# The order of TensorE's work in one recurrent step: the four groups of scores for the next step, placed one by one between groups of small products

## The chip, the cores and the metric

The kernel runs on one core of a Trainium2 chip. The metric is the device time of one execution in microseconds (us): the median of several runs, and, for one more execution, the time and the trace that the hardware profiler took.

## What is computed

One encoder layer over two sequences (1024 and 256 tokens, 1280 in all, width 1024): an input projection, a rotary attention branch, an RWKV-7 branch that reads the tokens forwards and backwards, a gated merge, and a feed-forward block with two layer norms. The part that the change touches is the recurrence of the RWKV-7 branch, for 16 heads of 64 in two directions:

```python
def step(S, inp):
    r_t, w_t, kh_t, ak_t, v_t, kt_t = inp
    sk = jnp.einsum('bhvk,bhk->bhv', S, kh_t)
    S = S * w_t[:, :, None, :] - sk[..., None] * ak_t[:, :, None, :] + v_t[..., None] * kt_t[:, :, None, :]
    return S, jnp.einsum('bhvk,bhk->bhv', S, r_t)
```

The kernel doesn't go token by token. It takes chunks of 64 tokens, in which the recurrence becomes products of 64x64 matrices and the inverse of a triangular matrix, and carries only the state S from chunk to chunk.

## The kernel before

The layer is done in stages, each with its own semaphores and a barrier at its end. The recurrence is `state_stage` (L1145 to L1445), some 457 us of the 3401 us. It walks 40 steps (`NSTEP`): 20 chunks for each half of the heads. One step works on 8 units (`U`), four forward and four backward, each a pair of heads. Nothing plans the order: each engine's instructions are written out by hand, and semaphores hold them against each other.

In one step g TensorE (PE) does, in this order, with 16 products in each group unless said otherwise (the trace counts an fp32 product as two MATMUL and two LDWEIGHTS):

- L1269 and L1235, mixed, 32 products: state times keys into bank BB, and the centred values of step g + 1 into bank UB;
- L1284: one corner of the inverse (called x here), into bank CB, which ACT evicts as Wt (L1349);
- L1293 and L1296, mixed, 32 products: the outputs' part from the state (bank OB) and the rest of BB; its last instruction raises `b_ready`, on which ACT evicts Bs (L1356) and the sync queue loads the operands of step g + 3 (L942, called at L1205, two DMAs of 640 KB);
- L1304: the second corner (n), on which DVE builds the inverse NF (L1392 and L1393, two of each);
- `scores(g + 1, 0)` and `scores(g + 1, 1)` (L1228), 4 products of 192 columns each;
- `heads` with NF and Bs (L1243), called u here; it ends in the eviction of X on ACT (L1361) and DVE (L1436);
- `scores(g + 1, 2)`;
- `heads` with KTt and X (L1243), called s: the change of the state, which DVE adds and scales (L1403, L1410);
- `scores(g + 1, 3)`;
- `heads` with X and SC (L1243), called o: the outputs, which DVE moves to oR (L1421, L1423).

A group of scores uses one of two pairs of PSUM banks, so `scores` waits until DVE's `mask` (L1380) and ACT's `transposes` (L1334) of the group two before are done. DVE goes through `inverse(g)`, `mask(g+1, 0)`, `mask(g+1, 1)`, the X eviction, `mask(g+1, 2)`, `state(g)`, `mask(g+1, 3)`, `outputs(g)`. ACT goes through Wt, the two halves of the values (`evict`, L1339), Bs, transposes 0 and 1, X, transposes 2 and 3. The sync queue loads the corners of the inverse for four further steps at every fourth step (L1195), behind `nf_done`.

Of the kernel before, what the change touches and what calls it, by code (L numbers as in the profile page):

```python
# [7 lines left out]
ALU = mybir.AluOpType  # L8
# [1136 lines left out]
def state_stage(nc, hbm, cst, pv, oR, ring, ahead, pool, ub_ready, xT, oa_ready):  # L1145

    with Stage(nc, "rc") as st:
        NSTEP = 2 * NCH
# [5 lines left out]
        NF = st.sb("NF", 128, U, CH)  # L1154
# [4 lines left out]
        ps = st.psum()  # L1159
# [18 lines left out]
        def nblk(g):  # L1178
            return 5 * (g // NCH) + (g % NCH) // 4
# [35 lines left out]
        def _(pe):  # L1215
# [42 lines left out]
            for g in range(NSTEP):  # L1258
                x, sc, v = ub[g % 3], SC[g % 2], X[g % 2]
                if g + 1 < NSTEP:  # L1260
                    pe.wait_ge(ub_ready[(g + 1) % 3], 32 * ((g + 1) // 3) + 32)
                    if g:
                        pe.wait_ge(u_done, 2 * g)
                    else:
                        pe.wait_ge(v_done, 2)
                pe.wait_ge(s_done, 2 * g + 2)
                for u in range(U):
                    for h in range(2):
                        last = pe.matmul(ps[half(h), BB, CH * u:CH * u + CH], x[half(h), u, 3 * CH:4 * CH], S[half(h), u, :],  # L1269
                                         start=u == 0, stop=True, skip_group_check=True)  # L1270
                    if u == U - 1:
                        last.then_inc(bd_ready, 1)
                    if g + 1 < NSTEP:
                        values(g + 1, u)
                pe.wait_ge(masked, 4 * g + 4)
                pe.wait_ge(nb_ready[nblk(g) % 3], 64 * (nblk(g) // 3) + 64)
                if g:
                    pe.wait_ge(nf_done, 4 * g)
                n_, r_ = corners(nb, g), corners(rb, g)
                for u in ALTERNATE:  # L1280
                    for h in range(2):
                        d = u // 4
                        i, o = (64 * h, 64 * h + 32) if d == 0 else (64 * h + 32, 64 * h)
                        last = pe.matmul(ps[o:o + 32, CB, 32 * u:32 * u + 32], sc[i:i + 32, u, h, o % 64:o % 64 + 32],  # L1284
                                         r_[d][i:i + 32, u % 4, :], start=True, stop=True)
                last.then_inc(x_ready, 1)
                pe.wait_ge(v_done, 2 * g + 2)
                pe.wait_ge(bd_ready, g + 1)
                if g:
                    pe.wait_ge(o_done, 2 * g)  # L1290
                for u in range(U):
                    for h in range(2):
                        pe.matmul(ps[half(h), OB, CH * u:CH * u + CH], S[half(h), u, :], x[half(h), u, 4 * CH:5 * CH],  # L1293
                                  start=u == 0, stop=True, skip_group_check=True)
                    for h in range(2):
                        last = pe.matmul(ps[half(h), BB, CH * u:CH * u + CH], sc[other(h), u, h, 0:CH], v[other(h), u, h, :],  # L1296
                                         start=False, stop=True, skip_group_check=True)
                last.then_inc(b_ready, 1)
                pe.wait_ge(w_done, g + 1)
                for u in ALTERNATE:  # L1300
                    for h in range(2):
                        d = u // 4
                        i, o = (64 * h + 32, 64 * h) if d == 0 else (64 * h, 64 * h + 32)
                        last = pe.matmul(ps[o:o + 32, CB, 256 + 32 * u:256 + 32 * u + 32], Wt[i:i + 32, u, :],  # L1304
                                         n_[d][i:i + 32, u % 4, :], start=True, stop=True)
                last.then_inc(n_ready, 1)
                if g + 1 < NSTEP:
                    scores(g + 1, 0)
                    scores(g + 1, 1)
                    pe.wait_ge(v_done, 2 * g + 4)  # L1310
                pe.wait_ge(b_done, g + 1)
                pe.wait_ge(nf_done, 4 * g + 4)
                heads(ps, UB, lambda u, h: NF[half(h), u, :], lambda u, h: Bs[half(h), u, :], True).then_inc(u_ready, 1)
                if g + 1 < NSTEP:
                    scores(g + 1, 2)
                pe.wait_ge(u_done, 2 * g + 2)
                if not last_of(g):
                    pe.wait_ge(kt_done, 4 * g + 4)
                    heads(ps, BB, lambda u, h: KTt[g % 2][:, u, h, :], lambda u, h: v[:, u, h, :], True).then_inc(s_ready, 1)
                if g + 1 < NSTEP:  # L1320
                    scores(g + 1, 3)
                heads(ps, OB, lambda u, h: v[:, u, h, :], lambda u, h: sc[:, u, h, CH:2 * CH], False).then_inc(o_ready, 1)

        def score_view(ps, q, c, n):
# [4 lines left out]
        @block.scalar  # L1329
        def _(act):  # L1330
            def transposes(g, q):
                n = 4 * g + q
                act.wait_ge(masked, n + 1)
                act.activation(KTt[g % 2][:, 2 * q:2 * q + 2, :, :], score_view(ps, q, 128, CH), ACT.Copy).then_inc(kt_done, 1)  # L1334

            def evict(g):
                for h in range(2):
                    rows = slice(64 * h, 64 * h + 64)
                    act.activation(X[g % 2][rows, :, 1 - h, :], ps[rows, UB, :].rearrange("p (u n) -> p u n", n=CH),  # L1339
                                   ACT.Copy).then_inc(v_done, 1)  # L1340

            for q in range(4):
                act.wait_ge(sc_ready, q + 1)
                transposes(0, q)
            act.wait_ge(v_ready, 1)
            evict(0)
            for g in range(NSTEP):
                act.wait_ge(x_ready, g + 1)
                act.activation(Wt[:, :, :], ps[:, CB, 0:256].rearrange("p (u n) -> p u n", n=32), ACT.Copy, scale=-1.0).then_inc(w_done, 1)  # L1349
                if g + 1 < NSTEP:  # L1350
                    act.wait_ge(v_ready, g + 2)
                    if g:
                        act.wait_ge(o_ready, g)
                    evict(g + 1)
                act.wait_ge(b_ready, g + 1)
                act.activation(Bs[:, :, :], ps[:, BB, :].rearrange("p (u n) -> p u n", n=CH), ACT.Copy).then_inc(b_done, 1)  # L1356
                if g + 1 < NSTEP:
                    for q in range(2):
                        transposes(g + 1, q)
                act.wait_ge(u_ready, g + 1)  # L1360
                act.activation(X[g % 2][0:64, :, 0, :], ps[0:64, UB, :].rearrange("p (u n) -> p u n", n=CH),  # L1361
                               ACT.Copy, scale=-1.0).then_inc(u_done, 1)
                if g + 1 < NSTEP:
                    transposes(g + 1, 2)
                    transposes(g + 1, 3)

        @block.gpsimd
# [5 lines left out]
        def _(dve):  # L1373
# [6 lines left out]
                dve.tensor_tensor(SC[g % 2][:, 2 * q:2 * q + 2, :, :], score_view(ps, q, 0, 2 * CH),  # L1380
                                  cst[:, at:at + 128].unsqueeze(1).unsqueeze(1).broadcast_to([128, 2, 2, 128]), ALU.mult).then_inc(masked, 1)

            def inverse(g):
                n = corners(nb, g)
                dve.wait_ge(nb_ready[nblk(g) % 3], 64 * (nblk(g) // 3) + 64)
                dve.wait_ge(n_ready, g + 1)
                if g:
                    dve.wait_ge(u_ready, g)
                for d in range(2):
                    us, mine = slice(4 * d, 4 * d + 4), 1 - d  # L1390
                    z = ps[:, CB, 256 + 128 * d:384 + 128 * d].rearrange("p (u n) -> p u n", n=32)
                    dve.tensor_scalar(NF[:, us, 32 * d:32 * d + 32], n[d], sel[d], None, ALU.mult).then_inc(nf_done, 1)  # L1392
                    dve.scalar_tensor_tensor(NF[:, us, 32 * mine:32 * mine + 32], n[d], sel[mine], z, ALU.mult, ALU.add).then_inc(nf_done, 1)  # L1393

            def state(g):
# [32 lines left out]
            for q in range(4):  # L1428
                mask(0, q)
            for g in range(NSTEP):  # L1430
                inverse(g)
                if g + 1 < NSTEP:
                    mask(g + 1, 0)
                    mask(g + 1, 1)
                dve.wait_ge(u_ready, g + 1)
                dve.tensor_scalar(X[g % 2][64:128, :, 1, :], ps[64:128, UB, :].rearrange("p (u n) -> p u n", n=CH),  # L1436
                                  -1.0, None, ALU.mult).then_inc(u_done, 1)
                if g + 1 < NSTEP:
                    mask(g + 1, 2)
                state(g)  # L1440
                if g + 1 < NSTEP:
                    mask(g + 1, 3)
                if g:
                    dve.wait_ge(o_done, 2 * g)
                outputs(g)  # L1445
# [727 lines left out]
```

## Time and profile before

| | us |
|---|---|
| median of 3 runs | 3413.84 |
| the 3 runs | 3404.06, 3413.84, 3415.73 |
| the profiled execution | 3403.2 |
| its span in the trace | 3401.3 |
| PE busy in the span | 3227.4 (95%) |
| DVE busy | 1803.5 (53%) |
| ACT busy | 1035.7 (30%) |
| mean granted TensorE clock | 0.986 |

Times in the trace count from the start of the span. An idle stretch that the profile calls "issue" is one in which the engine waited for no other engine's work. PE and PEld are the MATMULs and the LDWEIGHTS of the same engine.

### The profile page before, as it was taken

The page shows a single profiled execution, that of the slowest core. Times are in us where ns is not written, and L with a number is a line of the kernel's source. Part 1 is how long each engine was busy: PE and PEld are TensorE (multiplying, and loading weights), DVE is VectorE, ACT ScalarE, POOL GpSimd, SP SyncE. Part 2 cuts the span into 40 slices and gives each one's busy share as a digit, 9 for nine tenths or more (in the row PEclk, how much of TensorE's full clock was granted, in tenths as well). Part 3 has the DMA queues.
Part 4 walks back from the last instruction along what each step waited for, and adds up shares of the span by engine and source line. Part 5 has one row for each costly group of instructions (what it writes and reads, how often), then busy time and mean ns, then how long its engine had stood idle before and what let it go on. Part 6 is the DMA issues. An engine that isn't in the chain of part 4 may idle for free. (4 is left out here: it accounts for less than half of the span.)

```text
span 3401.3 us, 59585 instructions
## 1 busy us (share of the span) xinstructions
PE 3227.4 (95%) x25992; PEld 2055.7 (60%) x25992; DVE 1803.5 (53%) x3002; ACT 1035.7 (30%) x1590; POOL 2.5 (0%) x13
## 2 busy tenths in 40 slices
PE   9999999999999899888888999998999999999997
PEld 4565564555555455577777554565666666666665
DVE  1437662677677478055555332155545445645445
ACT  2336651343333133233333452002321121221111
POOL 0000000000000000000000000000000000000000
PEclk9999999999999999999999999998999999999998
DMA  3221111344434423355443223211111211222211
GB/s 136 62 68 36 38 38 42 120 135 167 152 120 150 157 102 138 133 188 164 147 150 114 82 87 138 81 50 50 62 62 62 81 62 64 73 87 75 68 62 62
DMA packets 211234, 328.48 MB, mean 97 GB/s; under 512 B 51232, under 2 KB 168224, under 8 KB 205856
## 3 DMA queue, kind: packets, MB, share of 16 engines
q1 hardware_dynamic: 210976, 324.67, 28.7%
q8 instruction: 207, 3.39, 0.4%
q14 instruction: 51, 0.42, 0.0%
HBM read 221.74 MB, written 96.34 MB: 94 GB/s over the span
## 5 line engine op out<-in xcount | busy, mean ns | idle before, releaser
L620 PE MATMUL ra_ps<-xT,ring 128*128 128x512 f32 (+1 forms) x1152 | 429.8, 526 | 0.0
L1742 PE MATMUL tl_ps<-merged,pool 128*128 128x320 f32 x1440 | 407.4, 435 | 6.4 <-PEq L108 3.9
L1742 PEld LDWEIGHTS tl_ps<-merged,pool 128*128 128x128 f32 x1440 | 275.0, 191 | 124.0 <-issue 12.1
L620 PEld LDWEIGHTS ra_ps<-xT,ring 128*128 128x128 f32 x1152 | 214.3, 190 | 198.9 <-issue 189.3
L1935 DVE TENSOR_TENSOR oR<-tl_ps,oR 128x320 f32<-128x320 f32 x416 | 201.9, 489 | 151.2 <-PE tl_ps L1742 149.0
L1058 PE MATMUL rg_ps<-xT,ring 128*128 128x512 f32 (+1 forms) x720 | 265.7, 524 | 11.9 <-PEq L108 11.9
L1742 PE MATMUL tl_ps<-tl_Th,pool 128*128 128x320 f32 x720 | 205.7, 437 | 6.1 <-issue 6.1
L1058 PEld LDWEIGHTS rg_ps<-xT,ring 128*128 128x128 f32 x720 | 134.7, 191 | 122.7 <-issue 117.2
L1823 ACT ACTIVATE ring<-tl_ps 128x320 f32<-128x320 f32 x96 | 41.9, 437 | 528.7 <-PE tl_ps L1742 528.6
L1742 PE MATMUL tl_ps<-xT,pool 128*128 128x320 f32 x640 | 183.2, 433 | 0.0
L1941 DVE TENSOR_TENSOR merged<-tl_ps,ring 128x320 f32<-128x320 f32 x96 | 47.2, 491 | 254.0 <-PE tl_ps L1742 135.4
L1742 PEld LDWEIGHTS tl_ps<-tl_Th,pool 128*128 128x128 f32 x720 | 138.5, 193 | 64.7 <-issue 8.7
L1742 PE MATMUL tl_ps<-merged,tl_sums 128*128 128x320 f32 x544 | 163.2, 439 | 12.8 <-DVE oR L1935 7.8
L280 PE MATMUL at_ps<-xT,ring 128*128 128x512 f32 (+1 forms) x432 | 159.1, 521 | 0.0
L1228 PE MATMUL rc_ps<-pool 64*128 64x192 f32 x1280 | 142.5, 349 | 11.7 <-POOL pool L1370 6.9
L1742 PEld LDWEIGHTS tl_ps<-xT,pool 128*128 128x128 f32 x640 | 122.0, 191 | 51.1 <-issue 0.8
L1520 PE MATMUL mg_ps<-xT,ring 128*128 128x512 f32 (+1 forms) x384 | 144.2, 529 | 1.9 <-PEq L108 1.9
L305 PE MATMUL at_ps<-at_qk 128*128 128x512 f32 (+1 forms) x288 | 135.7, 594 | 8.3 <-ACT at_p L372 7.9
L1520 PE MATMUL mg_ps<-oR,ring 128*128 128x512 f32 (+1 forms) x384 | 139.4, 526 | 2.9 <-DVE oR L1573 2.9
L317 PE MATMUL at_ps<-at_turned,at_v 32*128 32x256 f32 x2176 | 137.0, 386 | 4.0 <-DVE at_ot L456 4.0
L1742 PEld LDWEIGHTS tl_ps<-merged,tl_sums 128*128 128x128 f32 x544 | 102.9, 192 | 62.0 <-issue 22.4
L317 PEld LDWEIGHTS at_ps<-at_turned,at_v 32*128 32x128 f32 x2176 | 108.3, 184 | 49.1 <-issue 43.4
(239 smaller groups left out, 4654.2 us busy)
## 6 DMA issues: line engine op xcount, KB each, us to landing
pool<-ub SPq DMA_DIRECT2D x80, 640.0 KB, 5.3
ub<-ra_ub SPq DMA_DIRECT2D x32, 1280.0 KB, 5.3
pool<-in_w_ff SPq DMA_DIRECT2D x32, 1024.0 KB, 4.7
pool<-in_w_ff SPq DMA_DIRECT2D x64, 512.0 KB, 3.5
ring<-in_w_in SPq DMA_DIRECT2D x39, 512.0 KB, 3.7
xT<-in_xT SPq DMA_DIRECT2D x16, 640.0 KB, 8.2
ub<-ra_v SPq DMA_DIRECT2D x16, 640.0 KB, 6.5
mg_gate<-gates SPq DMA_DIRECT2D x16, 640.0 KB, 3.9
```

What stands on the lines that cost most here:

```text
L280: last = pe.matmul(ps[:, z_bank(i) + j, 0:n], w[:, i % 3, 128 * k:128 * k + 128], xT[:, k, t0:t0 + n], start=(k == 0), stop=(k == KT - 1))
L305: last = pe.matmul(ps[:, 2 * (t % 2) + b // 512, 0:n], qk[:, h, t0:t0 + 128], qk[:, QH + h // (QH // KVH), k0 + b:k0 + b + n], start=True, ...
L317: last = pe.matmul(ps[:, 4 + i, 0:256], values_of(g, i, j), pT[g % 2][32 * i:32 * i + 32, j].rearrange("p t q -> p (t q)"), start=(j == 0) ...
L620: last = pe.matmul(ps[:, bank + j, 0:n], w[c][:, 128 * i:128 * i + 128], xT[:, i, t0:t0 + n], start=(i == 0), stop=(i == KT - 1))
L1058: last = pe.matmul(ps[:, 3 * (b % 2) + j, 0:n], w[b % 3][:, 128 * i:128 * i + 128], xT[:, i, t0:t0 + n], start=(i == 0), stop=(i == KT - 1))
L1228: last = pe.matmul(ps[:, 4 + 2 * (q % 2) + h, 192 * j:192 * j + 192], x[rows, 2 * q + j, CH:3 * CH], x[rows, 2 * q + j, 3 * CH:6 * CH], st ...
L1520: last = pe.matmul(ps[:, 3 * (i % 2) + j, 0:n], w[i % 2][:, 128 * k:128 * k + 128], src[:, k, t0:t0 + n], start=(k == 0), stop=(k == KT - 1))
L1742: last = pe.matmul(bank(n, b), lhs(k), rhs(k), start=(fresh and k == 0), stop=(k == d - 1), skip_group_check=True)
L1823: act.activation(cp[n % 2][:, c, :], bank(n, b), ACT.Copy).then_inc(done, 1)
L1935: dve.tensor_tensor(y, bank(n, b), y, ALU.add).then_inc(done, 1)
L1941: dve.tensor_tensor(hidden(n, i, j), bank(n, b), cp[n % 2][:, c, :], ALU.add).then_inc(done, 1)
```

## The change

Within a step, PE's groups stand in another order. x moves ahead of the group BB with values. The groups of scores for step g + 1 stand apart: 0 ahead of x, 1 between BB with values and OB with BB, 2 between n and u, 3 between u and s. s and o now follow each other, and so do x and the BB group. One explicit wait on `ub_ready` goes away, because `scores(g + 1, 0)` has the same. No product is added or removed.

DVE and ACT follow this order. `inverse(g)` is split: the two operations on the own corners (L1392), which need nothing of this step's products, go first; the two on the other corners (L1393) go behind the masks 0 and 1. Masks 2 and 3 come one place earlier, transposes 0 and 1 stand around `evict`, transposes 2 ahead of X.

```diff
             for g in range(NSTEP):
                 x, sc, v = ub[g % 3], SC[g % 2], X[g % 2]
                 if g + 1 < NSTEP:
-                    pe.wait_ge(ub_ready[(g + 1) % 3], 32 * ((g + 1) // 3) + 32)
+                    scores(g + 1, 0)
+                pe.wait_ge(masked, 4 * g + 4)
+                pe.wait_ge(nb_ready[nblk(g) % 3], 64 * (nblk(g) // 3) + 64)
+                if g:
+                    pe.wait_ge(nf_done, 4 * g)
+                n_, r_ = corners(nb, g), corners(rb, g)
+                for u in ALTERNATE:
...
+                last.then_inc(x_ready, 1)
+                if g + 1 < NSTEP:
                     if g:
                         pe.wait_ge(u_done, 2 * g)
...
                         last.then_inc(bd_ready, 1)
                     if g + 1 < NSTEP:
                         values(g + 1, u)
-                pe.wait_ge(masked, 4 * g + 4)
...
-                last.then_inc(x_ready, 1)
+                if g + 1 < NSTEP:
+                    scores(g + 1, 1)
                 pe.wait_ge(v_done, 2 * g + 2)
...
                 last.then_inc(n_ready, 1)
                 if g + 1 < NSTEP:
-                    scores(g + 1, 0)
-                    scores(g + 1, 1)
+                    scores(g + 1, 2)
                     pe.wait_ge(v_done, 2 * g + 4)
...
                 if g + 1 < NSTEP:
-                    scores(g + 1, 2)
+                    scores(g + 1, 3)
                 pe.wait_ge(u_done, 2 * g + 2)
...
-                if g + 1 < NSTEP:
-                    scores(g + 1, 3)
                 heads(ps, OB, lambda u, h: v[:, u, h, :], lambda u, h: sc[:, u, h, CH:2 * CH], False).then_inc(o_ready, 1)
...
                 if g + 1 < NSTEP:
+                    transposes(g + 1, 0)
                     act.wait_ge(v_ready, g + 2)
...
                     evict(g + 1)
+                    transposes(g + 1, 1)
                 act.wait_ge(b_ready, g + 1)
...
-                    for q in range(2):
-                        transposes(g + 1, q)
+                    transposes(g + 1, 2)
...
                 if g + 1 < NSTEP:
-                    transposes(g + 1, 2)
                     transposes(g + 1, 3)
...
-                inverse(g)
+                own_corners(g)
                 if g + 1 < NSTEP:
                     mask(g + 1, 0)
                     mask(g + 1, 1)
+                other_corners(g)
+                if g + 1 < NSTEP:
+                    mask(g + 1, 2)
                 dve.wait_ge(u_ready, g + 1)
...
                 if g + 1 < NSTEP:
-                    mask(g + 1, 2)
+                    mask(g + 1, 3)
                 state(g)
-                if g + 1 < NSTEP:
-                    mask(g + 1, 3)
```

## Rows read from the trace of the kernel before

**Rows 1.** The page's first part: busy time, share of the span, instructions.
```profile
PE 3227.4 (95%) x25992; PEld 2055.7 (60%) x25992; DVE 1803.5 (53%) x3002; ACT 1035.7 (30%) x1590; POOL 2.5 (0%) x13
```
**Rows 2.** Windows, steps 1 to 38: length, busy time (count) per engine, clock, DMA share, GB/s.
```profile
1456.20:1883.66 427.46, 371.94 (x12068) 321.86 (x12065) 237.99 (x530) 155.49 (x342) 0.00 (x0) 1.00 0.45 145
```
**Rows 3.** Waits of PE and PEld in these 38 steps: us in total, times, longest.
```profile
PE rc_ps L1296 <- issue: 16.2, 12, 1.7
...
PE rc_ps L1304 <- issue: 13.0, 9, 1.8
...
PE rc_ps L1293 <- issue: 8.6, 6, 1.8
...
PEld rc_ps L1243 <- DVE rc_X L1436: 8.4, 35, 0.2
```
**Rows 4.** Timeline of PE, one step: start, us, line, count, idle before.
```profile
1603.27 0.45 PE L1304 MATMUL rc_ps<-rc_nb,rc_Wt 32*32 32x32 f32 x32
1603.65 1.57 PE L1228 MATMUL rc_ps<-pool 64*128 64x192 f32 x16
1605.15 1.15 PE L1243 MATMUL rc_ps<-rc_Bs,rc_NF 64*64 64x64 f32 x32
1606.23 0.92 PE L1228 MATMUL rc_ps<-pool 64*128 64x192 f32 x8
1607.10 1.15 PE L1243 MATMUL rc_ps<-rc_X,rc_KT 128*64 128x64 f32 x32
1608.18 0.92 PE L1228 MATMUL rc_ps<-pool 64*128 64x192 f32 x8
1609.03 1.15 PE L1243 MATMUL rc_ps<-rc_SC,rc_X 128*64 128x64 f32 x32
1610.11 0.27 PE L1269 MATMUL rc_ps<-rc_S,pool 64*64 64x64 f32 x2
...
1611.20 0.45 PE L1284 MATMUL rc_ps<-rc_rb,rc_SC 32*32 32x32 f32 x32
1611.59 0.27 PE L1293 MATMUL rc_ps<-pool,rc_S 64*64 64x64 f32 x2
```
**Rows 5.** Windows from the end of one stall to the end of the next.
```profile
1467.52:1470.98 3.46, 2.20 (x127) 1.96 (x127) 0.00 (x0) 1.45 (x3) 0.00 (x0) 1.00 0.02 5
1490.81:1494.25 3.44, 2.16 (x127) 1.92 (x127) 0.00 (x0) 1.45 (x3) 0.00 (x0) 1.00 0.32 128
...
1757.81:1764.40 6.59, 5.82 (x125) 4.88 (x125) 5.03 (x11) 1.63 (x5) 0.00 (x0) 1.00 1.05 327
```
**Rows 6.** DMA queues in the 38 steps: packets, MB, share of 16 engines.
```profile
q8 instruction: 95, 1.56, 1.4%
```
**Rows 7.** DMA queues, 1468.60 to 1470.95 us.
```profile
q8 instruction: 1, 0.02, 2.8%
```
**Rows 8.** DMA queues, 1757.90 to 1762.10 us: all of them.
```profile
q1 hardware_dynamic: 1178, 1.37, 98.9%
q14 instruction: 1, 0.01, 0.5%
```
**Rows 9.** DMA queues, 1762.10 to 1764.35 us.
```profile
q8 instruction: 1, 0.02, 2.6%
```
**Rows 10.** Timeline of the sync queue: issues of the operand loads, 1755 to 1775 us.
```profile
1756.80 0.91 SPq L942 DMA_DIRECT2D pool<-ub  x2
```
**Rows 11.** Timeline of the sync queue, 1602 to 1605 us.
```profile
1603.37 0.92 SPq L942 DMA_DIRECT2D pool<-ub  x2
```
**Rows 12.** DMA queues, 1604.20 to 1604.40 us.
```profile
q8 instruction: 1, 0.02, 44.5%
```
**Rows 13.** Timeline of DVE in the step of rows 4.
```profile
1604.06 0.34 DVE L1393 SCALAR_TENSOR_TENSOR rc_NF<-rc_nb,cst,rc_ps 128x128 f32<-128x128 f32 x1
...
1604.52 0.34 DVE L1393 SCALAR_TENSOR_TENSOR rc_NF<-rc_nb,cst,rc_ps 128x128 f32<-128x128 f32 x1
...
1606.35 0.69 DVE L1436 TENSOR_SCALAR rc_X<-rc_ps 64x512 f32<-64x512 f32 x1 [0.29 <-PE rc_ps L1243]
...
1609.02 0.76 DVE L1410 TENSOR_TENSOR rc_S<-rc_t,pv 128x256 f32<-128x256 f32 x2
```

More of the change, by code:

```diff
@@ L1260, in _ @@
                 if g + 1 < NSTEP:
-                    pe.wait_ge(ub_ready[(g + 1) % 3], 32 * ((g + 1) // 3) + 32)
+                    scores(g + 1, 0)
[5 more added lines that the diff above has]
+                for u in ALTERNATE:
+                    for h in range(2):
+                        d = u // 4
+                        i, o = (64 * h, 64 * h + 32) if d == 0 else (64 * h + 32, 64 * h)
+                        last = pe.matmul(ps[o:o + 32, CB, 32 * u:32 * u + 32], sc[i:i + 32, u, h, o % 64:o % 64 + 32],
+                                         r_[d][i:i + 32, u % 4, :], start=True, stop=True)
+                last.then_inc(x_ready, 1)
+                if g + 1 < NSTEP:
                     if g:
@@ L1274, in _ @@
                         values(g + 1, u)
-                pe.wait_ge(masked, 4 * g + 4)
[L1276 to L1285, printed above, removed]
-                last.then_inc(x_ready, 1)
+                if g + 1 < NSTEP:
+                    scores(g + 1, 1)
                 pe.wait_ge(v_done, 2 * g + 2)
@@ L1381, in mask, with own_corners @@
                                   cst[:, at:at + 128].unsqueeze(1).unsqueeze(1).broadcast_to([128, 2, 2, 128]), ALU.mult).then_inc(masked, 1)
-            def inverse(g):
+            def own_corners(g):
                 n = corners(nb, g)
                 dve.wait_ge(nb_ready[nblk(g) % 3], 64 * (nblk(g) // 3) + 64)
-                dve.wait_ge(n_ready, g + 1)
                 if g:
@@ L1389, in inverse, with other_corners @@
                 for d in range(2):
+                    dve.tensor_scalar(NF[:, 4 * d:4 * d + 4, 32 * d:32 * d + 32], n[d], sel[d], None, ALU.mult).then_inc(nf_done, 1)
+            def other_corners(g):
+                n = corners(nb, g)
+                dve.wait_ge(n_ready, g + 1)
+                for d in range(2):
                     us, mine = slice(4 * d, 4 * d + 4), 1 - d
                     z = ps[:, CB, 256 + 128 * d:384 + 128 * d].rearrange("p (u n) -> p u n", n=32)
-                    dve.tensor_scalar(NF[:, us, 32 * d:32 * d + 32], n[d], sel[d], None, ALU.mult).then_inc(nf_done, 1)
                     dve.scalar_tensor_tensor(NF[:, us, 32 * mine:32 * mine + 32], n[d], sel[mine], z, ALU.mult, ALU.add).then_inc(nf_done, 1)
```

## Prediction

> **What bounds the kernel now.** I read the page's busy shares first: PE is busy for 95% of the span, DVE for 53% [rows 1], so time is won or lost on PE. The change touches only the recurrent stage. There the windows view gives 427.46 us for 38 steps, 11.25 us each, with PE busy for 371.94 of them at full clock [rows 2]: 55.5 us are idle. The view of waits says on what: nothing that another engine owed. Most of it is "issue", ahead of L1296, L1304 and L1293, at up to 1.8 us a time, and the only engine that PE's weight loads wait for is DVE's X eviction, 8.4 us in 35 times [rows 3].
>
> The timeline of a step without a stall gives each group's price as the distance of two starts [rows 4]: n 0.38, scores 0 and 1 together 1.50, u 1.08, scores 2 0.87, s 1.08, scores 3 0.85, o 1.08, BB with values 1.09, x 0.39, and OB with BB 1.09, taken as for the other mixed group, which has as many products. The sum is 9.41 us. The real step is 11.25, so about 1.84 us of each, 70 us of the stage, are stalls.
>
> What they are: from the end of one stall to the end of the next PE ran 127 MATMULs and 127 LDWEIGHTS, which with two waits are 256 instructions [rows 5], and the 38 steps have 95 packets on the DMA queue of instructions, 1.56 MB or 16 KB each [rows 6], which is 256 instructions of 64 bytes. PE is waiting for its own program. Two such stalls ended 3.44 and 3.46 us apart [rows 5], with one packet between them [rows 7]: entering a block asks for the next, and that is there some 3.5 us later. A step has 640 instructions and about 8 waits, 2.5 blocks.
>
> The Trainium skill's page Runtime: NRT & Kernel Launch, section Instruction fetch mechanics, also has 16 KB blocks fetched while the current one runs, and calls the cost of a boundary "mostly hidden". The trace agrees on the block and not on the cost. If it were hidden here, a step would take its 9.41 us, and of this change only the fourth tail (below) would be left, some 8 us slower.
>
> Second, a refill can be late. At 1756.80 the loads of step g + 3 are issued [rows 10]; PE enters a block at 1757.81, and its refill doesn't start before 1762.10: up to there only the load moves, on 98.9% of the DMA engines, and then the one packet of 16 KB comes [rows 8, 9]. That block took 6.59 us [rows 5]. A refill asked for at 1603.27, 0.1 us ahead of a load's issue [rows 4, 11], started 0.8 to 1.0 us behind that issue [rows 12]. Free of load it would start 1.1 to 1.3 us after the entry and be usable 2.3 us after that. So one that would start up to 1.0 us after the issue goes through, and one that would start at 2.2 us (1757.81 + 1.2 - 1756.80) waits until 5.3 us and is usable at 7.7. Where in between the line lies, the trace doesn't show.
>
> **The change part by part.**
>
> *The groups themselves.* No product is added. But a group of scores costs 0.64 us for its products and 0.22 until the next kind can start: two together take 1.50, one alone 0.86 [rows 4]. Before there are three such tails in a step, after it four: +0.22 us, 9.63 us without stalls. From below, the tail could cost nothing ahead of the small 32x32 products of x: no row has scores ahead of them. I take 0.2, since all three followers in the trace show it.
>
> *The removed wait* on PE is free, since the same wait stands in scores 0, and the loads were issued more than two steps earlier.
>
> *The waits that move.* u now has only scores 2 ahead of it (0.86) where it had 1.50. It waits for DVE: the second L1393 ended at 1604.86, 1.59 after n started, with four operations [rows 4, 13]. With two of them left behind n, the end comes some 0.4 us earlier, about 1.2 after n's start, where scores 2 ends at 0.38 + 0.86 = 1.24. That is covered by nothing to spare; its price lies between 0 and 0.1 us a step. s waits for X behind one group of scores as before (0.2 us at most, as now). The state is done at 1609.78, 0.33 ahead of its reader [rows 4, 13]; after the change o, scores 0 and x stand there, 2.3 us, so this cover grows and gives nothing, since PE isn't waiting there now. DVE's masks 0 and 1 stand ahead of the other corners, but score group 1 ends 1.5 us ahead of n's end, and a mask takes 0.7. On ACT transposes 0 and 1 stand ahead of Bs; they wait for the same masks and are done ahead of `b_ready` or within 0.2 us of it, and Bs is needed 1.2 us behind it. The loads hang on `b_ready` and those of the corners on `nf_done`, as before.
>
> *The stalls.* This is what the change really moves. In the dense stretch a block of 256 instructions before takes 2.0 us (BB with values, x, half of OB with BB), against 3.5 for the refill: 1.5 us of stall. After, scores 1 stands in it, and the same stretch takes 2.7 to 2.8: some 0.75 less. But the groups that follow the load have lost what the dense stretch won. From the end of OB with BB to the start of the next BB group before there are 325 instructions and 6.84 us; after, up to the start of x, there are 310 and 6.25 us, and then the dense groups start. A refill that the load holds up is usable at 7.7 us. Before, PE can be near that point with 256 instructions; after it gets there sooner.
>
> One walk by these two rules shows it. A block is entered 90 instructions behind OB with BB, in the shadow of the load. Before: the next block is wanted at 7.0 and is there at 7.7, stall 0.7; the one after is wanted 2.0 later, stall 1.5; two blocks on, 1.3; then 0 and 1.5 (5.0 us in three steps). After: wanted at 6.45, stall 1.25; then 0.7; 0.3 and 0.4; 0.9 and 0.75 (4.3 us in three steps). Three steps before: 28.2 + 5.0 = 33.2. After: 28.9 + 4.3 = 33.2. What the dense stretch gains, the held-up refill and the fourth tail take.
>
> I carried the same two rules through 39 steps for 32 positions of the first block boundary, with the hold lasting to 6.6 us in those steps that also load corners or attention outputs. Before gives 11.18 us a step, where the trace has 11.25; that is the check of the rules. After depends on the line between 1.0 and 2.2 us that the trace leaves open: up to 1.7 it gives 11.40 to 11.42 (+0.23), at 1.9 it gives 11.19 (0), at 2.17 it gives 10.95 (-0.23). With the line evenly likely between the ends, the mean is +0.14. Times 39 steps that is +5.5 us, with ends of -9 and +9.
>
> **The sum.** The profiled execution has 3403.2 us, 10.6 below the median of 3413.84; it is the fastest of the four times, whose spread is 12. With +5.5 its time is 3409. Against the median I forecast 3419.
>
> **The rivals.**
>
> *A, clearly faster: the load doesn't hold these refills.* If each refill takes 3.5 us wherever it is asked for, the rules give 10.55 before and 10.03 after: -0.52 us a step, -20 us, 3394. For it: the dense stretch is the largest stall in rows 3, and the change thins just that. Against it: before would be at 10.55, not 11.25, and rows 8 to 10 show the hold. A part of this is possible, where the line lies at 2.2 or a held refill gets through earlier: -10 to -12, 3402. The Trainium skill's page DMA: Bandwidth & Descriptors, section Queues, rings and completion order, has each DMA engine take turns between its queues packet by packet; by that a refill wouldn't wait for a whole load. Rows 8 and 9 show one that did.
>
> *B, clearly slower: the shadow of the load begins early, and u waits.* The line is at 1.7 or below (+0.23), and u pays its 0.1 for the corners: +0.33 us a step, +13, 3427. It decides from the point where the other corners end over 1.24 us after n's start.
>
> *C, DVE or ACT in a new order becomes the bound.* DVE is busy 238 of 427 us, ACT 155 [rows 2]. Were a mask or Bs 0.5 us late in each step, +20, 3434. I see no place for it: little chance.
>
> *D, nothing of this matters,* stalls are as before and the tail is absorbed in them: 3414, inside my forecast.
>
> **How the numbers follow.** About 0.3% (10 us) is what a measurement of this kernel can tell from no change. Forecast and D (within it): 0.45. A, full or in part: 0.24. B and C: 0.31. The range holds the forecast, the part of A down to half its price and B: 3398 to 3434.
>
> **What would show it.** In the trace after: the step without a stall is 9.6 us; scores stand in four places with 0.86 each; the "issue" waits ahead of L1296, L1293 and L1304 shrink by about half, and those ahead of L1284, L1269, L1235 and of o grow by about as much; the 38 steps take 427 to 437 us. If the latter don't grow, A is right. If u's weight loads wait for DVE L1393, B's part is right. The prediction is wrong if the stage's time moves by over 12 us, or if other stages do.

## The result, and the profile after

The changed kernel takes 3418.26 us (median of 20 runs, 3411.13 to 3426.45). The kernel before, run beside it on the same chip, takes 3410.24 (median of 20 runs, 3404.06 to 3426.57). The ratio is 1.0028 with an interval of 1.0019 to 1.0036: slower by 0.28%, some 8 to 10 us. That is just under the 0.3% that I had named as the limit of what can be told apart, and the interval lies clear of 1.

The profiled execution took 3417.64 us, with a span of 3415.8. Its page's first part, to be held against [rows 1]:

```profile
PE 3236.4 (95%) x25992; PEld 2062.6 (60%) x25992; DVE 1810.0 (53%) x3002; ACT 1041.2 (30%) x1590; POOL 2.5 (0%) x13
```

The same instructions ran, as they should. Now the recurrent stage, from the barrier ahead of it to the one behind it, in the windows view (stretch, length, busy time and count of PE, PEld, DVE, ACT, POOL, granted clock, DMA share, GB/s). First before, then after:

```profile
1433.70:1894.00 460.30, 395.58 (x12672) 342.24 (x12672) 251.16 (x559) 163.86 (x360) 1.72 (x3) 0.98 0.46 148
```
```profile
1431.30:1915.40 484.10, 412.80 (x12672) 350.75 (x12672) 257.27 (x559) 169.31 (x360) 1.72 (x3) 0.95 0.44 141
...
1458.78:1909.08 450.30, 388.34 (x12020) 330.42 (x12017) 242.62 (x527) 158.95 (x338) 0.00 (x0) 0.95 0.43 138
```

The stage is 23.8 us longer in this pair of profiles, and the other stages together 9.3 shorter, which makes the 14.5 between the spans. The other stages run the same code in all 14 profiles below, and what is left of the span beside the recurrent stage ranges from 2931.7 to 2942.2 us in them, so the 9.3 is scatter. The second row of after is 38 steps, from n of one to n of another: 450.3 us, where [rows 2] has 427.46. The last figure but two is what surprises: the granted clock is 0.95, where [rows 2] has 1.00. I come back to it; it isn't in my sum at all.

The waits of PE in those 38 steps (us in total, times, longest), against [rows 3]. The lines have moved: L1271 is x, L1282 BB, L1235 values, L1296 OB with L1299, L1307 n, L1243 u, s and o.

```profile
PE rc_ps L1282 <- issue: 12.5, 9, 3.6
PE rc_ps L1235 <- issue: 8.2, 5, 3.4
PE rc_ps L1299 <- issue: 7.5, 11, 1.5
PE rc_ps L1271 <- issue: 7.4, 8, 1.3
PE rc_ps L1228 <- issue: 6.9, 4, 3.1
PE rc_ps L1296 <- issue: 6.3, 5, 2.5
PE rc_ps L1243 <- issue: 5.8, 7, 1.6
PE rc_ps L1307 <- issue: 5.3, 5, 1.6
```

The lines of before that [rows 3] leaves out, from the same stretch:

```profile
PE rc_ps L1269 <- issue: 6.6, 5, 2.3
PE rc_ps L1228 <- issue: 4.5, 6, 1.2
PE rc_ps L1284 <- issue: 3.5, 4, 1.3
PE rc_ps L1235 <- issue: 1.5, 3, 0.9
PE rc_ps L1243 <- issue: 0.9, 1, 0.9
```

In [rows 3] three lines had 37.8 us of the 54.8 that this view puts down to "issue". L1299, L1307 and L1296 answer to them and fell from 16.2, 13.0 and 8.6 to 7.5, 5.3 and 6.3. x, BB, values and the L1243 groups rose from 3.5, 6.6, 1.5 and 0.9 to 7.4, 12.5, 8.2 and 5.8. So the first fell by 18.7 us and the others rose by 21.4, as the prediction had named it ("by about as much"). But the longest stalls are now 3.1 to 3.6 us, ahead of BB, values and scores, where the longest of before in this stretch was 2.3.

A step without a stall, as the timeline of PE shows it (start, us, line, count):

```profile
1591.15 0.45 PE L1307 MATMUL rc_ps<-rc_nb,rc_Wt 32*32 32x32 f32 x32
1591.53 0.92 PE L1228 MATMUL rc_ps<-pool 64*128 64x192 f32 x8
1592.43 1.15 PE L1243 MATMUL rc_ps<-rc_Bs,rc_NF 64*64 64x64 f32 x32
1593.51 0.92 PE L1228 MATMUL rc_ps<-pool 64*128 64x192 f32 x8
1594.37 1.15 PE L1243 MATMUL rc_ps<-rc_X,rc_KT 128*64 128x64 f32 x32
1595.35 1.10 PE L1243 MATMUL rc_ps<-rc_SC,rc_X 128*64 128x64 f32 x32
1596.38 0.92 PE L1228 MATMUL rc_ps<-pool 64*128 64x192 f32 x8
1597.23 0.45 PE L1271 MATMUL rc_ps<-rc_rb,rc_SC 32*32 32x32 f32 x32
```

The scores stand alone, 0.85 to 0.90 each. s and o now follow each other directly and take 2.01 together (1594.37 to 1596.38), where each took 1.08 in [rows 4]. Over the groups of all steps that had no stall in them, a step without stalls comes to 9.50 us, where before has 9.41.

*How the stalls were split.* In every profile below I counted PE's instructions in blocks of 256 from the known boundary. The boundary falls on the same place of the count in all of them, since the instructions are as many. For each block I noted when it was entered, when the next packet on the queue of instructions started, and how long PE then stood at the next boundary. A refill whose packet started over 1.6 us after the entry is called held, whatever held it; the others are called free. The stage of before has 24.4 us of stalls behind held refills and 45.5 behind the others. The stage of after has 62.8 and 14.1. So of the stalls that the change was to thin, two thirds are gone, and the others have grown 2.6-fold.

One of the long ones. The sync queue issues the loads, PE enters a block at 1552.21, and only the operand loads' queue moves up to 1558.20 (DMA queues of 1552.30 to 1558.20 us, then of 1558.20 to 1560.50; packets, MB, share of 16 engines):

```profile
1549.65 1.56 SPq L942 DMA_DIRECT2D pool<-ub  x2
1551.26 0.51 SPq L1210 DMA_DIRECT2D xT<-o_att  x1
```
```profile
q1 hardware_dynamic: 910, 1.57, 77.9%
...
q8 instruction: 1, 0.02, 2.5%
```
```profile
1560.55 0.37 PE L1282 MATMUL rc_ps<-rc_S,pool 64*64 64x64 f32 x2 [3.58 <-issue]
```

This is the picture of [rows 8, 9], with the attention load queued as well, and with the dense groups right at its end. PE stands for 3.58 us, inside BB.

### The profile page after: what moved, and what is told of

The parts are those of the page before. It is cut to its first block and busy times, and to the rows that moved or that the text cites. A ratio compares the mean times of both kernels' runs of the same rounds, so it can differ in the third digit from the quotient of the medians.

```text
span 3415.8 us, 59584 instructions
## 1 busy us (share of the span) xinstructions
PE 3236.4 (95%) x25992; PEld 2062.6 (60%) x25992; DVE 1810.0 (53%) x3002; ACT 1041.2 (30%) x1590; POOL 2.5 (0%) x13
## 3 DMA queue, kind: packets, MB, share of 16 engines
q1 hardware_dynamic: 210976, 324.67, 28.5%
## 5 line engine op out<-in xcount | busy, mean ns | idle before, releaser
L1747 PEld LDWEIGHTS tl_ps<-merged,pool 128*128 128x128 f32 x1440 | 275.3, 192 | 123.4 <-issue 11.9
L1380 DVE TENSOR_TENSOR rc_SC<-rc_ps,cst 128x512 f32<-128x512 f32 x160 | 110.3, 689 | 117.3 <-PE rc_ps L1228 117.3
L1228 PE MATMUL rc_ps<-pool 64*128 64x192 f32 x1280 | 157.3, 365 | 14.3 <-POOL pool L1370 6.9
```

The lines of the kernel that those rows point to most:

```text
L1228: last = pe.matmul(ps[:, 4 + 2 * (q % 2) + h, 192 * j:192 * j + 192], x[rows, 2 * q + j, CH:3 * CH], x[rows, 2 * q + j, 3 * CH:6 * CH], st ...
L1747: last = pe.matmul(bank(n, b), lhs(k), rhs(k), start=(fresh and k == 0), stop=(k == d - 1), skip_group_check=True)
```

## The experiments

All times are medians, and the ratio behind each is to the kernel before, run beside it on the same chip. The table gives, from one profile of each kernel, the stage's length, the two kinds of stalls in it, the stalls over 2 us, and the length of the spells at a granted clock of 0.50 that begin in it. A profile is one execution: those of before_paced and after_early took 3418.0 and 3380.6 us, 7.5 over and 9.1 under their medians, so their rows are less typical than the others.

| kernel | median us | stage | held | others | over 2 us | clock at 0.50, us |
|---|---|---|---|---|---|---|
| before | 3410.2 | 460.3 | 24.4 | 45.5 | 2 | 17.0 |
| before_again | (3412.6) | 472.2 | 29.0 | 42.4 | 4 | 37.4 |
| after | 3418.3 | 484.1 | 62.8 | 14.1 | 9 | 44.2 |
| after_again | (3418.5) | 481.6 | 61.7 | 17.9 | 9 | 30.6 |
| before_cut | 3364.9 | 423.2 | 0.2 | 36.2 | 0 | 13.6 |
| after_cut | 3346.0 | 409.5 | 6.4 | 13.9 | 1 | 3.4 |
| before_half | 3425.9 | 491.8 | 43.0 | 20.4 | 3 | 47.6 |
| before_paced | 3410.5 | 473.6 | 40.5 | 28.5 | 11 | 51.0 |
| after_paced | 3380.0 | 436.8 | 29.9 | 14.0 | 2 | 6.8 |
| after_spread | 3380.4 | 439.9 | 27.8 | 18.7 | 2 | 6.8 |
| after_poolq | 3429.8 | 489.5 | 67.9 | 14.5 | 14 | 40.8 |
| after_fine | 3378.2 | 436.3 | 28.4 | 16.4 | 2 | 3.4 |
| before_early | 3407.3 | 464.0 | 33.5 | 30.5 | 8 | 40.8 |
| after_early | 3389.7 | 443.3 | 34.8 | 15.4 | 3 | 6.8 |

In brackets: one execution.

**Take the load away: before_cut and after_cut.** Both orders of PE, but the loads of the steps move almost no bytes: the operands' (shown), and in the same way those of the corners and of the attention outputs. The recurrence's result is left out, and its instructions stay.

```diff
...
-                    load_units(sp, hbm, ub[g % 3], g + 3, ub_ready[g % 3])
+                    for d in range(2):
+                        sp.dma_start(ub[g % 3][0:16, 4 * d, 0:5 * CH],
+                                     hbm["ub"][0, d, 0:16, chunk_of(g % 3, d), :]).then_inc(ub_ready[g % 3], 16)
...
```

> The kernel before, with the sync queue's DMAs inside the 40 steps cut to 16 partitions (operands of later steps, corners, attention outputs), the operands and corners of the first three steps used again, and the new state multiplied by a zero column, so that nothing grows: the recurrence's result is left out, its instructions stay. Theory (refills of PE's program held behind the loads): no refill is held, a step takes 10.55 us instead of 11.24, so some 27 us less than the kernel before; the stalls behind BB with values (1.5 us each in OB with BB and n) stay. Rival (the stalls have nothing to do with the loads): the time of the kernel before within 5 us.

> The same cut on the changed kernel. Theory: with no refill held, the thinner dense stretch pays at last: 9.86 us a step against 10.55, so 27 us LESS than before_cut, some 50 less than the kernel before. Rival (the change costs time by its fourth tail of a scores group and by waits for DVE and ACT): 5 to 15 us MORE than before_cut.

Measured: before_cut 3364.91 (ratio 0.986, 0.9843 to 0.9877), 43 us under before; after_cut 3346.04 (0.9806, 0.9789 to 0.9823), 19 under before_cut and 72 under after. Their stages in the windows view:

```profile
1436.60:1859.80 423.20, 387.03 (x12672) 336.94 (x12672) 250.70 (x559) 163.63 (x360) 1.72 (x3) 0.98 0.09 24
```
```profile
1435.90:1845.40 409.50, 391.00 (x12672) 334.62 (x12672) 256.99 (x559) 167.37 (x360) 1.72 (x3) 0.99 0.09 25
```

The DMA share is down from 0.46 to 0.09, held stalls are gone in the first and down to 6.4 us in the second (what holds those I didn't find), and now the change pays: 19 us. With the loads in place it costs 8 to 10. So the loads take some 28 us off what the new order brings by itself. That is the core of my theory, and the direction of the theory holds on both sides. Both sizes were off. Before lost 43 instead of 27. One part of that is the stalls behind free refills, which shrank too (45.5 to 36.2), and which my fixed 3.5 us didn't allow; with the held ones that makes 33.5, and the rest isn't explained. The change brought 19 instead of 27, which is what the prediction had put under rival A (20).

**Spread the load: before_paced and after_paced.** Four pieces of 320 KB, one each behind OB with BB, u, o and the next BB group.

```diff
-                    load_units(sp, hbm, ub[g % 3], g + 3, ub_ready[g % 3])
+                    piece(g, 0)
+                    sp.wait_ge(u_ready, g + 1)
+                    piece(g, 1)
+                    sp.wait_ge(o_ready, g + 1)
+                    piece(g, 2)
+                    sp.wait_ge(bd_ready, g + 2)
+                    piece(g, 3)
```

> The kernel before, complete, but each step's operand load is issued in four DMAs of 320 KB, at the ends of OB with BB, u, o and the next BB group, in place of two of 640 KB at the first of these. Theory: a refill then waits for one piece of some 1.2 us, not for 4; steps of 10.6 to 10.9 us, 13 to 25 us less than the kernel before. Rival: the kernel before within 5 us.

> The same pacing on the changed kernel, complete. Theory: steps of 9.9 to 10.4 us, 35 to 50 us less than the kernel before, and the granted clock stays at full in the stage since no stall is over 2 us. Rival: the changed kernel's 3418 within 5 us.

Measured: before_paced 3410.52 (1.0006, 0.9993 to 1.0018), after_paced 3380.0 (0.9906, 0.9891 to 0.9921). The windows view of the two:

```profile
1436.80:1910.40 473.60, 408.90 (x12672) 354.09 (x12672) 252.04 (x559) 164.87 (x360) 1.73 (x3) 0.95 0.50 144
```
```profile
1435.40:1872.20 436.80, 396.60 (x12672) 337.56 (x12672) 257.17 (x559) 168.56 (x360) 1.72 (x3) 0.99 0.54 156
```

The same bytes, with after in 47 us less of stage than when they come at once (38 in the medians), and before with no gain. For after the theory held in kind and was too high in size: I expected 35 to 50 us under before and steps of 9.9 to 10.4 us, and got 28 by the medians (32 by the ratio) and 38 steps in 406.7 us, 10.7 each. There were still two stalls over 2 us and 6.8 us at 0.50, where I expected none. For before it missed: I expected a gain and found none. The split shows what happened. The stalls behind free refills fell from 45.5 to 28.5, but the held ones rose from 24.4 to 40.5, eleven of them over 2 us, and the sum hardly moved (69.9 and 69.0). My reading is that the pieces behind o and BB come just where the dense stretch of before needs its refills, and that nothing long stands in that stretch to cover a late one; before_early below moves them and gains only 4 us, so this reading isn't shown.

**Half of the change: before_half.** The kernel before with only score group 0 moved, from behind n to between x and OB with BB. DVE and ACT keep their order.

```diff
+                if g + 1 < NSTEP:
+                    scores(g + 1, 0)
...
-                    scores(g + 1, 0)
```

> The kernel before with one part of the change alone: only scores 0 of the next step moves, from behind n to between x and OB with BB; ACT and DVE keep their order. Theory: stalls behind refills that no load holds fall (45.5 us before, 25 to 35 here), those behind held refills grow (24.4 us before, 35 to 50 here), for 310 instructions are left behind the load instead of 325; a step is 11.4 to 11.6 us, the time 5 to 15 us over the kernel before. Rival (stalls alone follow the dense stretch): both kinds of stall fall and the time is 5 to 10 us under the kernel before.

Measured: 3425.85 beside 3410.99 (1.0044, 1.0028 to 1.006), 15 us over before and slower than the whole change. That is the upper end of what I expected, but not for my reason alone. Its waits of PE name a cause that neither before nor after has:

```profile
PE rc_ps L1243 <- DVE rc_NF L1394: 12.5, 30, 0.4
...
PE rc_ps L1269 <- issue: 10.4, 10, 3.0
```

One group of scores is left between n and u, as in the whole change, but DVE still has all four operations on the corners behind n. So u waits for them in 30 of the steps, 12.5 us in total. In the whole change two of the four have gone ahead, and u waits for NF only once, in the first step (waits of after in its stage):

```profile
PEld rc_ps L1243 <- DVE rc_X L1443: 9.5, 38, 0.9
PEld rc_ps L1296 <- ACT rc_X L1339: 8.6, 33, 0.4
...
PE rc_ps L1271 <- DVE rc_SC L1380: 1.5, 1, 1.5
...
PE rc_ps L1243 <- DVE rc_NF L1397: 0.8, 1, 0.8
```

So this kernel doesn't isolate the refills, as I had meant it to. Held stalls of 43.0 are within the 35 to 50 that I expected and the others, 20.4, under the 25 to 35; what each part is worth in time can't be read from it. What it shows is that the wait of rival B exists, and that the split of `inverse` is what the whole change avoids it with.

**Spread the corner loads too: after_spread.** after_paced, with one of the four corner loads in each of four steps, issued behind the piece that follows u.

```diff
...
-                if g % 4 == 3 and nblk(g) + 3 < 10:
-                    sp.wait_ge(nf_done, 4 * g + 4)
-                    load_inverse(nblk(g) + 3)
+                    if g >= 3 and nblk(g - 3) + 3 < 10:
+                        h = g - 3 - (g - 3) % 4 + 3
+                        sp.wait_ge(nf_done, 4 * h + 4)
+                        load_inverse(nblk(h) + 3, (g - 3) % 4)
...
```

> after_paced, and the loads of the inverse's corners too are taken apart: one DMA of 256 KB in each of four steps in place of four behind each other in every fourth. Complete. Theory: steps 3, 7, ... 27 have the longest holds (packets up to 9 us behind the load's issue in the changed kernel), so these seven steps lose 1 to 2 us each: 3370 against 3380, no half clock in the stage. Rival (what is left is stalls of 3.5 us refills and tails only): 3380 within 3 us.

Measured: 3380.37 (0.9912, 0.9899 to 0.9925), the same as after_paced, where the theory had 3370. The rival was right: once the operand load is spread, the corner loads cost nothing that can be measured.

**The same two kernels again.** To see what one profile is worth.

> The kernel before once more, for its trace: the stage between its barriers took 460.3 us with 2 spells at half clock that are not its end. If these are typical, it is within 5 us of that; theory two (the first trace of before was a lucky one) has it at 465 to 475 us.

> The changed kernel once more, for its trace: the stage took 484.1 us, with 10 spells at half clock, 44 us. Theory (long stalls behind held refills let the clock drop): again 8 to 12 such spells and 478 to 488 us. If it was chance, 3 or fewer spells and some 470 us.

Measured: 3412.62 and 3418.51, 5.9 apart. The stage of before_again in the windows view:

```profile
1435.90:1908.10 472.20, 406.10 (x12672) 351.36 (x12672) 252.50 (x559) 164.69 (x360) 1.72 (x3) 0.96 0.46 145
```

It is 11.9 us longer than in the first profile of the same kernel, with nearly the same stalls (71.4 against 69.9). What differs is the clock: spells of 37.4 us at a granted 0.50 instead of 17.0, in six more of 3.4 us each, and the same instructions keep PE busy for 406.10 us instead of 395.58. So one spell costs some 1.7 us (the 10.4 that the stalls leave, over six), and the spells vary from run to run. The profile on which I built the prediction was a lucky one; against the second one the stage of after_again (481.6) is only 9.4 longer. In this second pair the stalls make +8.2 (held +32.7, others -24.5), the groups +3.5 (below) and two spells fewer some -3.4, which is 8.3 of the 9.4. after_again has 7 spells that begin in the stage, where the theory wanted 8 to 12; its stage lies in the range that I gave.

**Another engine's queue: after_poolq.** The operand loads of after, issued by GpSimd behind the same `b_ready`, and no longer by the sync engine.

```diff
...
+            for g in range(NSTEP - 3):
+                pool.wait_ge(b_ready, g + 1)
+                load_units(pool, hbm, ub[g % 3], g + 3, later[g % 3])
```

> The changed kernel, complete, with the operand loads of the 40 steps issued from GpSimd instead of the sync queue, at the same semaphore. It asks whose the hold is. If the DMA engines work off what is queued before the refill, whoever queued it: refills held as in the changed kernel, time 3410 to 3430. If only the sync queue's DMAs hold the refill: stalls behind held refills fall from 62 us to under 20 and the time to 3370 to 3385.

Measured: 3429.82 beside 3411.71 (1.005, 1.0036 to 1.0063), 67.9 us of held stalls. In the trace these loads stand on another DMA queue (q0 software_dynamic, 48.50 MB) than in all other kernels (q1). So the hold doesn't depend on which engine queues the load, nor on that queue; with the cut kernels it says that what holds is the load on the DMA engines. Why this kernel is 11 us slower than after isn't shown.

**Finer pieces: after_fine.** Eight of 160 KB, each behind another group.

```diff
...
+                    piece(g, 0)
+                    sp.wait_ge(n_ready, g + 1)
+                    piece(g, 1)
+                    sp.wait_ge(u_ready, g + 1)
+                    piece(g, 2)
...
+                    sp.wait_ge(bd_ready, g + 2)
+                    piece(g, 6)
+                    sp.wait_ge(sc_ready, 4 * (g + 2) + 2)
+                    piece(g, 7)
```

> The changed kernel, complete, each operand load in eight DMAs of 160 KB spread over the step (ends of OB with BB, n, u, scores 3, o, x, BB, scores 1). Theory: a refill waits for at most one piece of 0.6 us, stalls behind held refills fall from the 29.9 us of after_paced to some 15, time 3365 to 3375. Rival: with more pieces more refills meet one, and the time is 3380 or above.

Measured: 3378.2 (0.9905, 0.989 to 0.992). I expected 3365 to 3375. The held stalls stayed at 28.4 (29.9 in after_paced): half the piece doesn't mean half the hold. It is the fastest of the kernels that compute everything, level with after_paced and 0.95% under before, but it doesn't beat after_paced by anything that can be told.

**Pieces where the scores are: before_early and after_early.** Four pieces, all ahead of the dense stretch. In before they go out behind OB with BB, scores 1, u and scores 2. In after the same waits come true earlier than I had expected: scores 1 has long been done when the first piece goes out, and the last piece waits for scores 2, which in this order stands ahead of u. So the pieces go out in two pairs, two directly behind OB with BB and two directly behind u. In one step of the trace the issues stand at 1.7, 2.1, 4.1 and 4.5 us from the start of OB with BB, and u ends at 4.0.

```diff
+                    piece(g, 0)
+                    sp.wait_ge(sc_ready, 4 * (g + 1) + 2)
+                    piece(g, 1)
+                    sp.wait_ge(u_ready, g + 1)
+                    piece(g, 2)
+                    sp.wait_ge(sc_ready, 4 * (g + 1) + 3)
+                    piece(g, 3)
```

> The kernel before, complete, with the same four DMAs of 320 KB as before_paced, but issued at the ends of OB with BB, scores 1, u and scores 2, so that all are over before the dense stretch. before_paced issued the last at the end of BB with values, where its refills are. Theory: held stalls fall from before_paced's 40.5 us to 10 to 25, the others stay at 40 to 45; time 3395 to 3405, 5 to 15 us under the kernel before. Rival (splitting the load does nothing for this order wherever the pieces stand): 3408 to 3415.

> The changed kernel, complete, with the four DMAs of 320 KB issued at the ends of OB with BB, scores 2 (the second group's semaphore is long past, so directly behind the first piece), u and scores 3: the same pieces as after_paced, all within the first half of the step. It asks which part of the pacing pays for the changed order, that the load is split or that it is spread over the step. If the split pays, 3378 to 3385, as after_paced. If the spread pays too, since pieces close together are worked off as one load: held stalls of 35 to 50 us against 29.9, time 3388 to 3400.

Measured: before_early 3407.28 (0.9984, 0.9975 to 0.9993), after_early 3389.7 beside 3412.54 (0.9936, 0.9923 to 0.995). For before that is a little under 0.2%, between theory and rival; of the stalls, the held ones were 33.5, not 10 to 25, and the others 30.5, not 40 to 45. For after a load that comes in two halves, the second behind u, brings most of the gain (23 us under before), and four pieces over the whole step bring a further 9 or 10.

## Why the prediction was right, and where it was off

The forecast was 3419, the measured median is 3418.26, inside the range, and of the cases "within 0.3%" came true. That nearness is partly luck: I forecast +5.5 from a median of three runs (3413.84), and the change made +8 to +10 against one of twenty (3410.24). It is luck in a second way, too: by the sign that I had set myself, a stage that moves by over 12 us, the first pair of profiles (23.8) speaks against the prediction, and only the second pair (9.4) and the medians agree with it. By the steps:

*What bounds the kernel: right.* PE waits for its program, and the operand loads hold the refills. Taking the loads' bytes away took 43 us from before and 72 from after, and the held stalls fell to 0.2 and 6.4 us with them.

*The groups: +0.22 us a step predicted, +0.09 measured* (9.50 against 9.41). The fourth tail is there (0.85 from scores to x, as to any other kind). What I missed is the other side of the same move: s is now followed by o directly instead of by scores, and the pair takes 2.01 us where two groups took 2.16. That is 0.15 back. It hardly helps: carried again through 39 steps with the groups at 9.50, the two rules of the prediction give 11.41 us a step, and with 9.63 11.43 (an estimate, from the prices in [rows 4] and in the step above, the line at 1.3 us). By these rules, what the groups save, PE spends waiting for a refill that comes no sooner for it.

*The waits that move: right.* u waits visibly for DVE's corners once, for 0.8 us; otherwise it starts 0.90 us behind the start of the scores ahead of it, where the other groups start 0.85 to 0.86 behind theirs, which is within the 0 to 0.1 that I had. PE's weight loads wait 9.5 us for X in the stage, about as in [rows 3], and what else PE waits for on DVE is single events of at most 1.5 us. One wait is new, the weight loads of OB with BB for ACT's eviction of the values (8.6 us in 33 times). It costs nothing that can be seen, since from the scores ahead of that group to its start it is 0.85 us as elsewhere. C didn't come. before_half shows what the split of the corners is worth: without it u waits 0.4 us in most steps.

*The stalls: right in kind, too small in sum.* I had the dense stretch gain some 0.75 us a stall and the held refills eat it. Of my +0.14 a step the groups were +0.22, so the stalls as a whole were to fall by 0.08; with the line at 1.7 or below they were to stay (+0.01). Measured over the 39 steps, the stalls behind free refills fell by 31.4 us (0.81 a step), and those behind held ones rose by 38.4 (0.98 a step). The net is +7.0, or +0.18 a step (+8.2 us in the second pair). With the groups' +0.09 that makes +0.27 a step and 10.5 us for the stage. So the groups were forecast too dear and the stalls too cheap, and the two misses partly cancel. D, by which the stalls stay as they are, is only 4 us from the measured median, but both kinds of stall moved by over 30 us.

*The line that I left open* is the term that was mis-sized. I had it evenly between 1.0 and 2.2 us and took the mean, +0.14. In the trace after, the four refills that would have started 1.4 to 2.2 us behind the issue of the load started 5.0 to 5.4 us behind it. In the two traces of before and the two of after, 66 refills started in the first 1.3 us behind the issue of a load, three at 1.9 to 2.6, and none from there to 4.9. So the line lies between 1.0 and 1.4, which is the +0.23 case (9 us, where the medians show 8 to 10), and the one that I had put under rival B. Rival A (-20, the loads don't hold these refills) is what happens when they don't: after_cut against before_cut gained 19.

*The hold itself is longer than I had it* in the steps that also load corners or attention outputs: 8.4 to 9.0 us behind the end of OB with BB, where 8.0 was before's longest.

*The clock: not in the sum.* I had named as a sign that the 38 steps take 427 to 437 us and that the stage doesn't move by over 12. They took 450.3, and in that pair of profiles the stage moved by 23.8. Of the 23.8, 7.0 are stalls and 3.5 the groups; the rest, some 13, goes with 27 us more of granted clock at 0.50, the length of eight spells of 3.4 us, at the 1.7 us a spell that the two profiles of before show. Here is one, ahead of and after its start (windows view of after, the block of the long stall and the spell):

```profile
1552.20:1560.56 8.36, 4.77 (x127) 4.04 (x127) 4.49 (x10) 1.74 (x4) 0.00 (x0) 0.90 0.58 199
...
1558.80:1565.60 6.80, 5.05 (x127) 4.49 (x126) 0.69 (x1) 1.56 (x3) 0.00 (x0) 0.50 0.02 4
```

PE had been waiting since 1556.97 (1560.55 - 3.58) when the granted clock fell to 0.50, which is the lower of its two levels (1.2 GHz of 2.4). But in the second pair of profiles after had less of them than before (30.6 us against 37.4), and the other stages of after were 9 us faster in the first pair. What the two medians show, 8 to 10 us, is what the stalls and the groups explain without any clock. So I don't claim the spells as a cost of this change. They are a term that swings by 10 us and more between two executions of one kernel, and that I hadn't seen, since [rows 2] happened to have one of 3.4 us, which its 1.00 rounds away.

*The Trainium skill's page DMA: Bandwidth & Descriptors, section Queues, rings and completion order*, has the engines alternate between rings per packet. The trace doesn't agree: behind a load in one piece, the packet of instructions started 5.0 to 8.9 us after the load's issue, and with the load on GpSimd's queue just as on the sync engine's. The trace has only the packet's start, so whether the refill waits in its queue or is asked for late isn't shown. The Trainium skill's page Runtime: NRT & Kernel Launch, section Instruction fetch mechanics, calls boundaries "mostly hidden"; here they cost 70 to 80 us of the stage with the loads, and 20 to 36 without.

What stays open: where exactly the line lies between 1.0 and 1.4 us, why eight pieces hold no less than four, and what starts a clock spell. All 29 spells that begin in the stage in the two traces of before and the two of after do so during a stall of PE or at most 2 us behind its end, but these traces have 118 stalls of 1.2 us or more. Long stalls and spells go together in most kernels (two stalls over 2 us and one or two spells in the paced and fine ones, 9 and 10 in after), but before_again has eight short spells beside the one at the stage's end, and four such stalls.

## What to carry to other kernels

Where small float32 products run back to back and the profile shows "issue" ahead of them at intervals of 256 instructions, PE is waiting for its own program, and it matters which products stand between two block boundaries and which DMA is queued when a block is entered. Judge a reordering together with the loads: the new order here loses 8 to 10 us with the load in one piece and gains some 30 with the same bytes in four pieces spread over the step, while the old order gains nothing from them. And what the new order saves in its groups is worth little while PE waits for its program. And take a second profile before calling a stage's length a base: this one differed by 12 us between two executions of one kernel.

## What the runs showed of the hardware that I had not expected

- A block refill of 16 KB that would start 1.4 us or more behind the issue of 1280 KB of loads isn't served between their packets but behind them, from 5.0 us after the issue on, and up to 8.9 with further loads queued; the same with the loads on GpSimd's queue.
- In this stage the granted clock drops to 0.50 for 3.4 or 6.8 us at a time (10.2 at the end of the stage), 1 to 12 times in a profile, and a spell of 3.4 us costs about 1.7 us. Spells that begin outside the stage sum to 74 to 91 us in the 14 profiles.
- Two groups of 16 small products of the same line in a row (s, then o) take 0.15 us less together than with a group of scores between them.
- Without the loads, stalls behind refills that nothing held were shorter too, 36.2 us instead of 45.5.
